# Attention after four query projections instead of five, two weight splits on GpSimd in halves, and the compressed probabilities copied by ScalarE

## The reference

```python
k_cmp, v_cmp, k_slc, v_slc, k_win, v_win = kv      # 4 groups of 64
q = (h @ w_qg)[..., :1024] -> 16 heads of 64; gate = sigmoid(rest) -> 3 for each head
s_c = q @ k_cmp + bias; p_c = softmax(masked s_c); o_c = p_c @ v_cmp     # 15 compressed keys
s_s = q @ k_slc + bias; p_s = softmax(masked s_s); o_s = p_s @ v_slc     # selected keys (all, here)
s_w = q @ k_win + bias; p_w = softmax(masked s_w); o_w = p_w @ v_win     # window
o = g0 * o_c + g1 * o_s + g2 * o_w;   y = o @ w_o
k_cmp, v_cmp = gelu(blocks @ cmp_w1 + b1) @ cmp_w2
```

## Time and profile before

| | us |
|---|---|
| median of 3 runs | 636.45 (636.32 to 636.69) |
| the profiled execution | 635.05 |
| its span, first to last instruction | 633.3 |
| PE, DVE, ACT, POOL busy in it | 612.2, 485.3, 388.6, 59.4 |

### The profile page before, as it was taken

How to read it: one execution, slowest core, us unless ns; L and a number is a source line. 1 busy time by engine, 2 the same in 40 slices (tenths; PEclk the granted TensorE clock), 3 DMA queues, 4 the chain that set the end, 5 groups by cost and what they waited for, 6 DMA issues and landing times.

```text
span 633.3 us, 11277 instructions
## 1 busy us (share of the span) xinstructions
PE 612.2 (97%) x3738; PEld 531.8 (84%) x3738; DVE 485.3 (77%) x939; ACT 388.6 (61%) x708; POOL 59.4 (9%) x78
## 2 busy tenths in 40 slices
PE   7999999999999999999999888998999999999995
PEld 7999997888888888888989766777888888888884
DVE  4787756888888777777878789837788887777865
ACT  6645436666666666658556478717766666656644
POOL 0110011000000000011131144421000000000010
PEclk9999999999999999999999999999999999999999
DMA  8797432565655555761476400033355655555521
GB/s 313 283 334 241 181 132 100 184 212 198 203 200 199 184 182 181 290 224 35 148 255 206 136 2 2 1 101 132 138 209 190 219 205 193 178 175 186 199 100 66
DMA packets 30640, 109.55 MB, mean 173 GB/s; under 512 B 3419, under 2 KB 3691, under 8 KB 30476
## 3 DMA queue, kind: packets, MB, share of 16 engines
q1 hardware_dynamic: 30044, 106.97, 48.1%
q0 software_dynamic: 560, 2.12, 1.0%
HBM read 108.00 MB, written 1.07 MB: 172 GB/s over the span
## 4 chain that ended last, share of the span: by engine, by line
PE 88%; DVE 5%; ACT 3%; issue 2%; POOL 1%; DMA 1%; SPq 0%; DVEq 0%; ACTq 0%
PE bank L1109 26%; PE bank L1090 15%; PE bank L1091 14%; PE bank L1092 14%; PE bank L1110 13%; POOL work L486 1%; DMA staged<-in_a_up 1%; DVE work L1013 1%; PE bank L1356 1%; ACT work L533 1%; PE bank L1314 1%; PE bank L1144 1%; ACT w_hi L529 1%; PE bank L1316 0%; ACT L508 0%
## 5 line engine op out<-in xcount | busy, mean ns | idle before, releaser
L746 DVE TENSOR_TENSOR w_lo<-staged,w_hi 128x1024 fp32r<-128x1024 f32 x191 | 236.7, 1248 | 42.1 <-ACT w_hi L529 42.0
L1109 PE MATMUL bank<-gx,w_hi 128*128 128x512 f32 x704 | 249.7, 398 | 0.9 <-DVE gx L820 0.9
L529 ACT ACTIVATE w_hi<-staged 128x1024 fp32r<-128x1024 f32 x197 | 199.4, 1046 | 25.1 <-PE bank L1092 15.7
L1110 PE MATMUL bank<-gx,w_lo 128*128 128x256 f32 x704 | 197.7, 281 | 0.0
L1109 PEld LDWEIGHTS bank<-gx,w_hi 128*128 128x128 f32 x704 | 132.3, 188 | 33.0 <-issue 1.3
L1110 PEld LDWEIGHTS bank<-gx,w_lo 128*128 128x128 f32 x704 | 133.3, 189 | 1.5
L1091 PE MATMUL bank<-w_lo,y 128*128 128x512 f32 x208 | 81.6, 392 | 0.0
L1090 PE MATMUL bank<-w_hi,y 128*128 128x512 f32 x208 | 81.5, 392 | 0.0
L1092 PE MATMUL bank<-w_hi,y 128*128 128x512 f32 x208 | 81.0, 390 | 0.0
L615 ACT ACTIVATE work<-work,params 128x256 f32<-128x256 f32 x96 | 44.2, 504 | 56.9 <-DVE work L847 39.2
L1090 PE MATMUL bank<-gx,w_hi 128*128 128x256 f32 x256 | 72.9, 285 | 3.2 <-DVE w_lo L746 2.7
(11 more groups left out here) (156 smaller groups left out, 785.8 us busy)
## 6 DMA issues: line engine op xcount, KB each, us to landing
staged<-in_f_up SPq DMA_DIRECT2D x88, 512.0 KB, 5.2
staged<-in_f_down SPq DMA_DIRECT2D x44, 512.0 KB, 3.3
staged<-in_a_up SPq DMA_DIRECT2D x24, 512.0 KB, 7.0
staged<-in_b_up SPq DMA_DIRECT2D x24, 512.0 KB, 4.0
staged<-in_a_down SPq DMA_DIRECT2D x8, 512.0 KB, 3.4
staged<-in_b_down SPq DMA_DIRECT2D x8, 512.0 KB, 4.2
bias<-bias_rows POOLq DMA_DIRECT2D x1, 2048.0 KB, 12.0
bias<-in_xT SPq DMA_DIRECT2D x4, 256.0 KB, 5.5
```

Of the source, the lines that this page charges most:

```text
L529: nc.scalar.activation(w_hi[:, q["slot"], 0:n], staged[:, s, 0:n], ACT.Copy).then_inc(hi, 1)
L746: nc.vector.tensor_tensor(w_lo[:, q["slot"], 0:n], staged[:, s, 0:n], w_hi[:, q["slot"], 0:n].bitcast(F32), ALU.subtract).then_inc(lo, 1)
L1109: nc.tensor.matmul(out_ap, w_hi[:, s, cols], gx[:, kt, :], start=start, stop=False, skip_group_check=True)
L1110: return nc.tensor.matmul(out_ap[:, 0:T], w_lo[:, s, cols], gx_hi[:, kt, :], start=False, stop=stop, skip_group_check=True)
```

## The change

- `B_ORDER`: the last `w1` piece moves ahead of projection 1. `compressed()` moves from behind projection 3 to behind projection 2, on TensorE and on DVE.
- `Q_BEFORE` is 4: four projections come before attention. Projection 4 is computed between scores(0) and scores(1), projection 5 behind scores(1), projection 6 in cycle 3 instead of cycle 0, projection 7 stays in cycle 5. DVE moves projection 4 out before weigh(0) and projection 5 out in cycle 0.
- DVE no longer splits the pieces 26 and 27 (output pieces 1 and 2, `q_index(3) + 6` and `q_index(4) + 6`). POOL does it in halves of 512 columns after heads 5, 7, 9 and 11. ACT leads 26 before attention as before, 27 in cycle 0 instead of before attention, 28 in cycle 1, 29 in cycle 4 instead of cycle 2, 30 in cycle 5.
- The compressed probabilities `ends_T` are copied by ACT (`keep_ends`, after the exps and the lead of the odd head, before lead_heads). The last matmul pair of attend waits for it.

```diff
-Q_BEFORE = 5
+Q_BEFORE = 4
-           + [("w1", 0), ("gate", 0), ("w1", 1), ("q", 0), ("w1", 2), ("q", 1), ("w1", 3)] + ...
+           + [("w1", 0), ("gate", 0), ("w1", 1), ("q", 0), ("w1", 2), ("w1", 3), ("q", 1)] + ...
 # POOL
+            def rest_half(b, h):
+                q = piece_of("b", "up", b, 0)
+                cols = slice(h * 512, h * 512 + 512)
+                if h == 0:
+                    pool.wait_ge(hi_up, q["n"] + 1)
+                    pool.wait_ge(lo_up, q["n"])
+                r = nc.gpsimd.tensor_tensor(w_lo[:, q["slot"], cols], staged[:, q["slot"], cols],
+                                            w_hi[:, q["slot"], cols].bitcast(F32), ALU.subtract)
+                if h:
+                    r.then_inc(lo_up, 1)
+                if e in REST_AFTER:          # behind the compressed probabilities of head e
+                    rest_half(*REST_AFTER[e])
 # ACT
+            def keep_ends(i):
+                act.wait_ge(probs1, 2 * i + 2)
+                nc.scalar.activation(ends_T, bank[5][0:2 * 32, T:2 * T], ACT.Copy).then_inc(ends_kept, 1)
                     if h in LEAD_AFTER:
                         lead("b", "up", q_index(LEAD_AFTER[h]) + AHEAD, 0)
+                keep_ends(i)
                 lead_heads(i)
 # DVE
-                if (what, t) == ("q", 3):
+                if (what, t) == ("q", 2):
                     dve.wait_ge(cmp_mm, 1)
-                rest("b", "up", b + AHEAD, 0)
                 if (what, t) == ("q", Q_BEFORE - 1):
                     break
+                rest("b", "up", b + AHEAD, 0)
-                q = nc.vector.tensor_copy(probsT[:, g % 2, 512:768], bank[5][:, 0:T])
-                if g % 2:
-                    q = nc.vector.tensor_copy(ends_T, bank[5][0:2 * 32, T:2 * T])
-                q.then_inc(probs1, 1)
+                nc.vector.tensor_copy(probsT[:, g % 2, 512:768], bank[5][:, 0:T]).then_inc(probs1, 1)
-            query(5)
+            query(4)
+                if i == 0:
+                    query(5)
 # TensorE
-                    if t == 3:
+                    if t == 2:
                         compressed()
+                if g >= 2:
+                    pe.wait_ge(ends_kept, g // 2)            # in turn
+                pe.wait_ge(ends_kept, i + 1)                 # in attend, before its last pair
                 nc.tensor.matmul(bank[6][:, 0:T], vc[:, a, :], ends_T, ...)
             scores(0)
+            queries(4)
+            scores(1)
             queries(5)
-            scores(1)
-Q_CYCLE = {0: 6, 5: 7}
-LEAD_AFTER = {3: 5, 5: 6, 11: 7}
+Q_CYCLE = {3: 6, 5: 7}
+LEAD_AFTER = {1: 4, 3: 5, 9: 6, 11: 7}
+REST_AFTER = {5: (q_index(Q_BEFORE - 1) + AHEAD, 0), 7: (q_index(Q_BEFORE - 1) + AHEAD, 1),
+              9: (q_index(Q_BEFORE) + AHEAD, 0), 11: (q_index(Q_BEFORE) + AHEAD, 1)}
```

More of the change, by code:

```diff
@@ L59 @@
 B_ORDER = ([("cmp", t) for t in range(4)] + [("key", t) for t in range(4)] + [("val", t) for t in range(4)]
-           + [("w1", 0), ("gate", 0), ("w1", 1), ("q", 0), ("w1", 2), ("q", 1), ("w1", 3)] + [("q", t) for t in range(2, 8)]
+           + [("w1", 0), ("gate", 0), ("w1", 1), ("q", 0), ("w1", 2), ("w1", 3), ("q", 1)] + [("q", t) for t in range(2, 8)]
            + [("o", t) for t in range(8)])
@@ L251, in build @@
         turned0, turned1, probs0, probs1 = sem("turned0"), sem("turned1"), sem("probs0"), sem("probs1")
+        ends_kept = sem("ends_kept")
         headed, o_hi_done, o_lo_done = sem("headed"), sem("o_hi_done"), sem("o_lo_done")
@@ L1447 @@
 NOTHING = ([], [], [])
-AFTER_POOL = {("f0", "down", 0, 0), ("f0", "up", 2, 0), ("b", "up", 4, 0), ("f1", "down", 0, 0), ("f1", "up", 2, 0)}
+AFTER_POOL = {("b", "up", q_index(Q_BEFORE + 1) + AHEAD, 0), ("f0", "down", 0, 0), ("f0", "up", 2, 0), ("b", "up", 4, 0), ("f1", "down", 0, 0), ("f1", "up", 2, 0)}
 def UPS(st, k, i=0):
```

## The result

| | kernel before | changed kernel |
|---|---|---|
| median, 18 runs each | 636.07 us | 637.47 us |
| lowest and highest | 634.47 to 636.69 | 636.18 to 638.87 |
| profiled execution | 635.05 (span 633.3) | 636.18 (span 634.5) |

The ratio is 1.0026 with a 95% interval of 1.0019 to 1.0033: slower by 0.26%, some 1.65 us by the ratio and 1.4 by the medians. The forecast was 637.0, some 0.6 us slower than before; the direction is right, the size is not. The profiled executions lie 1.13 us apart, and 1.12 of it is there at project(0): from project(0) to the last instruction both take 224.5 us (633.3 - 408.83 and 634.5 - 409.95).

A forecast was written before the change was run, and what follows sets the result against it. ACT's closed loop bounds plain and lead cycles, PE turn(0) and projection cycles. Earlier entry brings 1.5 us, lighter cycles 0.75, three leads cost 2.85: 0.6 slower, 637.0 from median 636.45; range 634.4 to 638.2.

The forecast's parts named there:

- Part 1: Earlier entry into attention: scores(0) 2.34 us earlier, turn(0) 1.5 us earlier, at 362.15.
- the stall for `hid`: Behind projection 2, PE stands still for 0.6 us because compressed() needs hid, finished at 349.40.
- the first bias without a split ahead of it: Behind scores(0), DVE has no split left, so the first bias starts at 354.80, 3.03 us earlier.
- turn(0) bound by PE: Projection 5 ends at 362.15, after the chain's 360.63, so PE sets turn(0), 1.5 us earlier.
- Part 2: Copy of compressed probabilities moved from DVE to ACT: DVE loses 0.33 us per pair, a plain cycle gains only 0.10.
- the loop over ACT: Plain cycle: keep_turned, exps, copy, handoff, attend's last pair, turn, next keep_turned; sums to 6.42 us.
- The copy and its handoff: On ACT ahead of attend's last pair: copy 0.38 us plus handoff to PE 0.10, together 0.48.
- Part 3: Leads lose their cover in ACT's wait: 0.95 us each, making a cycle with a lead 7.37.
- Part 4: Two splits on GpSimd in halves of 1.20 to 1.5 us, hidden in its 2.33 us gaps; costed at nothing.
- turn(11) to project(0): End of attention: turn(11) to turn(13) 6.13 us, then 0.85; cycle 5's lead delays only turn(12), off the path.
- The faster rival: In attention's cycles the ACT loop does not bind and leads cost nothing: 2.26 us earlier, 634.2; chance 0.22.
- The slower rival: Copy and handoff take 0.75 us instead of 0.48 in cycles 0, 1, 2, 4: 638.1; chance 0.20.

The follow-up runs named there:

- first experiment: Changed kernel with ScalarE's copy of the compressed probabilities moved ahead of the lead instead of behind it; 633.6 us, ratio 0.996.
- third experiment: Kernel before with only the copy of the compressed probabilities moved to ScalarE, behind its lead; 637.61 us, ratio 1.0029.
- runs with a fill: Changed kernel with unused matmuls of ones on TensorE ahead of the wait for the copy, cycles 0, 1, 4: eight 639.9 us, four 636.88 us.

## Why the prediction was right in its direction and short in its size

Its own steps against the profiled execution of the changed kernel:

| step | forecast | measured |
|---|---|---|
| scores(0) | 353.09 | 353.18 |
| turn(0) | 362.15 | 362.32 |
| cycle 0, lead | 7.37 | 7.25 |
| cycle 1, lead | 7.37 | 7.60 |
| cycle 2, plain | 6.42 | 6.35 |
| cycle 3, projection | 8.19 | 8.18 |
| cycle 4, lead | 7.37 | 7.31 |
| turn(10) to turn(11) | 3.58 | 3.57 |
| turn(11) to turn(13) | 6.13 | 6.31 |
| turn(13) to project(0) | 0.85 | 1.06 |
| project(0) | 409.42 | 409.95 |

**Part 1** held, with turn(0) 0.17 late, of which 0.1 is there already ahead of the last two `w1` pieces: the stall for `hid` (0.6 forecast, 0.46 of idle time in the record), the first bias without a split ahead of it, turn(0) bound by PE. The run with the copy back on DVE has the earlier entry without the loss.

**Part 2** held: a plain cycle is 6.35. DVE's 0.33 us were on the chain of before, but the loop over ACT binds next; of the 0.33 only 6.52 - 6.35 = 0.17 comes through. That the loop binds in the plain cycle too is shown by the run with two copies. The copy and its handoff take 0.43, from 368.52 to 368.95, and not 0.48.

**Part 3** held, and it is the cause of the loss: moved behind the copy (first experiment) the leads cost nothing, and in the kernel before (third experiment) the same order makes the same 7.31.

**Part 4** held: halves of 1.29 us in gaps, nobody waits for them. The stretching that the table in the Trainium skill's "GPSIMD Engine Reference" (section "Specifications") allows for did not show: 1.27 to 1.30 for 512 columns is half of the 2.41 in the earlier trace rows and a fixed part. Its condition was not met either, since in these cycles DVE had no long instruction whose two inputs both lie in SBUF. The prediction asked only what POOL would suffer. In the kernel before it is DVE that got slower most: its split at 319.57, beside POOL's subtraction of the earlier trace rows and the addition behind it, took 2.86 us, and its split at 334.04, beside POOL's next subtraction, 2.57, where others take 1.22. In the cycles with POOL's halves DVE has no split, so nothing of this could arise; no run tests the halves beside one.

**What was too small.** The growth up to project(0) is 1.12 us and not 0.6. The step that failed is the last one, turn(11) to project(0): 7.37 measured, 6.98 forecast, 0.39 too little. I had said that the lead of cycle 5 delays turn(12) by some 0.3 and is "not on that path". The delay came (turn(11) to turn(12) is 4.87 against 4.60 before), and it is on the path twice. First, turn(13) waits 0.56 us for line 723: PE may write bank 4 for an odd head only when ACT has copied the even head's probabilities out of it, and that makes 6.31 of 6.13. Second, project(0) waits for DVE's last maximum, which stands behind a copy that waits for turn(12); it ends at 409.89, project(0) starts at 409.95, and that makes 1.06 of 0.85. I had counted ACT's lateness only against attend and the even turn.

The clock in cycle 1 adds some 0.3 (7.60 against 7.31 in cycle 4), which the forecast had no term for, and turn(0) 0.17. Against these stand cycles that are 0.06 to 0.12 shorter than forecast.

Beyond the one trace there is the spread of executions. Each one comes with its mean granted clock. At 0.995 and 0.996 the changed kernel's median is 637.17 us (7 executions of the 29 in two series) and that of the kernel before 636.12 (39 executions of 70): 1.05 us apart, close to the 1.12 of the two traces. The rest of the 1.4 goes with a lower mean clock, 0.993 against 0.996. Among the 29, the 15 executions below 0.994 have a mean time of 637.9, the 14 others of 637.0. The mean clock is a rough measure, since it also counts time at the end in which PE has nothing left to do (last section). The forecast moved the median by the shift of one profiled execution and had no term for this.

That 637.0 lies only 0.5 below the 637.47 measured is in part luck. It stood on a median of three runs, 636.45; the eighteen runs have 636.07. Against that the forecast shift of 0.6 is less than half of the measured 1.4. The prediction was too careful at another place: it took 0.2% as the least that can be told from no change, and the interval of the ratio is only 0.07% to each side.

The faster rival (leads hidden) did not come in the changed kernel, because the loop over ACT binds. It is what the kernel does once the copy stands first: 634.2 forecast, 633.6 measured. The slower rival (a dearer handoff) did not come, as the 0.43 says.

## What to carry to other kernels

Work moved from the busiest engine to a less busy one is free only where it stands in that engine's queue with nothing long ahead of it that nobody waits for: put what another engine waits for first and the long preparatory copy behind it. An idle gap on an engine hides a long instruction only as long as the gap is behind that instruction's place in the order; a new signal issued after it turns the cover into the critical path. When costing a late engine, list every wait on it, the reuse of a buffer too, not only the consumer that the change adds.

## What the runs showed of the hardware

The granted TensorE clock fell to 0.50 (1.2 of 2.4 GHz) for about three microseconds, while PE was at work, once or twice in ten of the thirteen traces, and at different places; the kernel before, the run with the copy back on DVE and the one with the Tanh earlier have no such fall. In the changed kernel, by windows of the trace:
```profile
368.00:371.00 3.00, 1.50 (x8) 0.96 (x9) 1.88 (x10) 2.01 (x5) 1.65 (x3) 0.97 0.00 0
371.00:374.00 3.00, 2.99 (x16) 2.50 (x18) 2.26 (x14) 3.00 (x14) 0.00 (x0) 0.50 0.02 5
```
PE was busy half of the three microseconds before, with the waits of 1.01 and 0.56 in them, and the turn at 371.01 takes 1.09 instead of 0.66. In the copy-first run the fall lies in the dense stretch before attention:
```profile
343.00:347.00 4.00, 4.00 (x23) 4.00 (x23) 3.79 (x11) 1.06 (x1) 0.00 (x0) 0.58 0.88 280
```
**What the fall costs** depends on who binds. In the changed kernel it cost 0.3 us, because PE's slower work took up the wait for ACT that stood at the end of the cycle. In the run with the copy on ScalarE alone it fell into cycle 3, which has no lead and no such wait, and that cycle took 7.68 us against the 6.36 of cycle 4: 1.3. In the copy-first run PE is the bound: turn(0) is 1.36 us later than in the changed kernel (363.68 against 362.32), of which 0.27 was there before the fall (the row ahead of the last two `w1` pieces is at 339.52 against 339.25); the wait of 0.46 for `hid` is taken up in it.

**Where it falls.** Six traces have PE waiting a microsecond or more for the late copy: both of the changed kernel, and the runs with the copy on ScalarE alone, the copy twice, the splits on DVE and the first one with the leads out. All six have one fall within 2.5 us behind such a wait, five of them at the start of the next odd turn and the sixth from 414.2 on. The seven others, both runs with a fill among them, have none between 362 and 420. It is one trace each, the fall comes once and not in every such cycle, and before the change waits of 0.99 in each plain cycle and 1.37 ahead of turn(0) brought none. So this, like the runs with the fill, says that the falls in attention go with the late copy; it does not show what sets one off. Six traces have a fall from about 11 to 14 us, at the start of the kernel. Ahead of it PE had waited 3.1 to 3.6 us for a split in five of them and 1.8 in the sixth; in the seven traces without it that wait was 1.5 to 2.5. For the two falls from 343 to 347 us, where PE was busy throughout, the runs give no reason.

**What the mean clock counts.** In the kernel before the only time at the low clock is from 630.5 us on, while PE's last matmul starts at 626.31. It costs nothing and still lowers the mean to 0.998. So two means of the clock can be compared only with this in mind.
